# Attention results turned by VectorE in squares of 32 instead of by TensorE

## The chip, the cores and the metric

The kernel runs on one core of a Trainium2 chip. The time is that of one execution on the device in microseconds (us); it is given as the median of several runs. PE is TensorE (matmuls, and PEld its weight loads), DVE is VectorE, ACT is ScalarE, POOL is GpSimd, SP issues the DMAs.

## The reference

256 tokens of 2048 channels go through one block with pooling and gated linear attention and a feed-forward layer, and then through two layers of a second block. The change lies in these two layers. Each computes, in float32:

```
h = rmsnorm(x);  z = h @ w_in                   # latents, conv inputs, q_mem, gate
q = rope(rmsnorm(q_lat) @ w_uq)                 # 8 heads of 128 + 64
k, v = rmsnorm(kv_lat) @ w_ukv
a_out = softmax(q k^T * scale) @ v              # 8 heads, v of 128 channels
c_out = gated convolution over 3 tokens         # 512 channels
m_out = softmax(q_mem mk^T * scale) @ mv        # 4 heads against 256 memory tokens
y = concat(a_out, c_out, m_out) * silu(gate)
x = x + rmsnorm(y @ w_o)
```

## The kernel before

**The stream.** Every product with a weight matrix is a group of k tiles (128 rows of weights, up to 512 columns). A float32 product is made of three matmuls of reduced precision: weights and activations are split into a high part (`wh`, a copy by ACT) and a low part (`wl`, the rest, by DVE), and PE computes high x high, low x high, high x low (L997 to L999). One k tile is a step; a 512-wide step is 6 matmuls for the two halves of 128 tokens. Weights are loaded in slabs of two k tiles, and there are four buffers of split slabs, so ACT may split a slab when PE has done the slab four before it. The results of a group lie in one of two PSUM accumulators, `pm`; a group may start when the group two before it has been taken out of PSUM (by ACT or DVE, as the group says).

**The background.** Everything else, attention too, is written on each engine as a generator that yields the step at which its next piece is due. On PE a piece due at step d is issued before step d. On ACT and DVE pieces are put between the splits of slabs; since these run ahead of PE, a piece due at step d stands before the split of the slab that begins six steps after d (d rounded up to even). All engines run their instructions in order, so a piece that waits holds all that is behind it.

**Attention.** A layer has 12 heads: 4 against the memory and then 8 of the sequence, two at a time (lanes `ln` 0 and 1), in six rounds r. `ROUNDS[r]` gives the steps one, two, three, four of a round, counted from the layer's first step L:

```python
ROUNDS = ((56, 60, 63, 69), (70, 74, 77, 81), (96, 100, 103, 107), (118, 122, 125, 129), (140, 144, 147, 151),
          (158, 162, 165, 169))
```

- one: PE computes the scores of both lanes into banks `pb` 4 and 5; DVE takes the row maxima (L1737), ACT the exponentials into `P` (L1096), with the sums; DVE their reciprocals.
- two: PE turns `P` (4 transposes of 128x128 for a lane, L654) into banks 6 and 7; DVE copies them to `PT` (L1746).
- three: PE multiplies by v (L836); DVE multiplies the result by the reciprocal and the gate and writes it over the first 128 columns of each half of `P` (L1755, due at three + 2; semaphore `ys`).
- four: PE turns this result, tokens on partitions, to channels on partitions (2 transposes for a lane); ACT copies it as the high part `yTh` (L1104, due at four + 1), DVE subtracts to get the low part `yTl` (L1557, due at four + 1).

`yT` is the activation of the last groups of a layer, `o`, which begin at step L + 184. The round of the last two heads is r = 5.

**Around it.** The groups of a layer are ql 0 to 15, kv, qm, gt3 48 to 63, uq0 64 to 67, gt0 68 to 83, uq1 84 to 87, ukv0 88 and 89, gt1 90 to 105, uq2 106 to 109, ukv1 110 and 111, gt2 112 to 127, uq3 128 to 131, ukv2, gc 134 to 149, ukv3 150 and 151, xi 152 to 167, gb, o. ACT takes out the gates gt (with a table load for Silu), uq (`s`, L1072), gc, and of ukv the values `vt` (L1138) and the high part of the keys `kT` (L1140); DVE takes the low part of the keys (L1846). DVE's rope of uq0 (L1684 to L1691) is due at step 68. Round r + 2 scores need `kT` of ukv r, so round 5's need that of ukv3. The feed-forward layer already turns its activations with DVE, in 16 instructions of 32 partitions x 256 elements (L1529), a block row of 4 at a time.

Of the kernel before, what the change touches and what calls it, by code (L numbers as in the profile page):

```python
# [7 lines left out]
F32 = mybir.dt.float32  # L8
F32R = mybir.dt.float32r
I32 = mybir.dt.int32  # L10
ACT = mybir.ActivationFunctionType
# [3 lines left out]
T = 256  # L15
# [256 lines left out]
def buffers(nc, ctx):  # L272
# [3 lines left out]
    def at(name, shape, off, dt=F32):  # L276
        return nc.alloc_sbuf_tensor_at(name, shape, dt, offset=base + int(off * 1024))

    def halves(name, nk, off_h, off_l):
        return at(name + "h", [128, nk, T], off_h, F32R), at(name + "l", [128, nk, T], off_l, F32R)  # L280
# [82 lines left out]
    m.vt = at("vt", [128, 2, 8, 128], RC + 36)  # L363
    m.gates = [at(f"gt{i}", [128, 2, 512], RC + 44 + 4 * i) for i in range(4)]
    m.S2 = [at(f"s2{i}", [128, 2, 512], RC + 60 + 4 * i) for i in range(2)]
    m.P = [at("P0", [128, 2, T], 4.5), at("P1", [128, 2, T], 6.5)]
    m.PT = [at("PT0", [128, 2, T], 8.5), at("PT1", [128, 2, T], 216)]
    m.kpeT = halves("kpeT", 1, 10.5, 218)
    m.kpd = at("kpd", [128, 2, 128], 218)
    m.rope_o = at("rope_o", [128, 2, 128], 219)  # L370
# [72 lines left out]
def ready(p, act, k, layer):  # L443

    if act in ("hT", "x2T", "xT3"):
        n = {"hT": 0, "x2T": 0, "xT3": 16 * (layer + 1)}[act]
        return ("hT_l" if act == "hT" else "xt_l"), n + k + 1
    if act in ("paT", "oT"):
        return act + "_l", k + 1
    if act == "mixT":  # L450
        return "mix_l", k // 2 + 1
    if act in ("memT", "memA", "memB"):
        return "mem_l", k // 4 + 1 if act == "memT" else {"memA": 4, "memB": 20}[act] + k + 1
    if act in ("qlT", "kvT"):
        return act[:2] + "_l", (4 if act == "qlT" else 2) * layer + k + 1
    if k in (8, 9, 10, 11):
        return "c_l", 2 * layer + (k - 8) // 2 + 1
    r, ln = ((k - 12) // 2, k % 2) if k >= 12 else (2 + k // 2, k % 2)
    return "y_l", 12 * layer + 2 * r + ln + 1


def sync_program(nc, s, m, a, cst, cpool, gains, out, p):
# [23 lines left out]
    def memory_again(n):  # L486

        for c in range(4):
            yield p.first[MEM_FROM[n]] + MEM_LOADS[n][c]
            if n:  # L490
                w.wait_ge(s["mm"], p.end["mv1"])
                w.wait_ge(s["yt_t"], 12)
            if c >= 2:
                w.wait_ge(s["mem_l"], 16 * n + 4 + 4 * (c - 1))
            elif n == 0 and c == 1:
                w.wait_ge(s["f_l"], 22)
            e.dma_start(m.memS[n][c % 2][:, :, :], a["memT"][:, 4 * c:4 * c + 4, :]).then_inc(s[f"d_m{c}"], 16)
# [140 lines left out]
def tensor_program(nc, s, m, p):  # L638
# [148 lines left out]
    def attention(l, r, which):  # L787

        idx = 2 * (6 * l + r)
        if which == 0:  # L790
            j = r % 2
            for ln in range(2):
                free(4 + ln)
            if r < 2:
                w.wait_ge(s["qm_l"], 2 * l + r + 1)
                w.wait_ge(s["mk_l"], l + 1)
                w.wait_ge(s["ev_a"], p.evac[f"mv{l}"])
                for ln in range(2):
                    h = 2 * r + ln
                    for qh in range(2):  # L800
                        o, qs = pb[4 + ln][:, qh * T:qh * T + T], slice(qh * 128, qh * 128 + 128)
                        e.matmul(o, m.qmT[0][:, h, qs], m.mkS[0][:, h, :], start=True, stop=False)
                        e.matmul(o, m.qmT[0][:, h, qs], m.mkS[1][:, h, :], start=False, stop=False)
                        ins = e.matmul(o, m.qmT[1][:, h, qs], m.mkS[0][:, h, :], start=False, stop=True)
                    ins.then_inc(s["sc"], 1)
            else:
                w.wait_ge(s["uq_l"], 4 * l + r - 1)
                w.wait_ge(s["uqr_l"], 2 * (4 * l + r - 1))
                w.wait_ge(s["kp_l"], l + 1)
                w.wait_ge(s["ev_d"], p.evac[f"ukv{l}{r - 2}"])  # L810
                (qh_, ql_), (kh_, kl_) = m.qT[j], m.kT[j]
                for ln in range(2):
                    for qh in range(2):
                        o, qs = pb[4 + ln][:, qh * T:qh * T + T], slice(qh * 128, qh * 128 + 128)
                        e.matmul(o, qh_[:, ln, qs], kh_[:, ln, :], start=True, stop=False)
                        e.matmul(o, qh_[:, ln, qs], kl_[:, ln, :], start=False, stop=False)  # L816
                        e.matmul(o, ql_[:, ln, qs], kh_[:, ln, :], start=False, stop=False)  # L817
                        e.matmul(o, m.qTr[j][ln][:, 0, qs], m.kpeT[0][:, 0, :], start=False, stop=False)  # L818
                        ins = e.matmul(o, m.qTr[j][ln][:, 0, qs], m.kpeT[1][:, 0, :], start=False, stop=True)
                    ins.then_inc(s["sc"], 1)  # L820
        if which == 1:
            for ln in range(2):
                free(6 + ln)
                w.wait_ge(s["ex"], 2 * (idx + ln) + 2)
                for kk in range(2):
                    ins = turn(6 + ln, kk, [m.P[ln][:, qh, kk * 128:kk * 128 + 128] for qh in range(2)])
                ins.then_inc(s["pt_t"], 1)
                bank[6 + ln] = ("pt_c", idx + ln + 1)
        if which == 2:
            for ln in range(2):  # L830
                h = 2 * r + ln if r < 2 else 2 * (r - 2) + ln
                w.wait_ge(s["pt_c"], idx + ln + 1)
                for qh in range(2):
                    for kk in range(2):
                        v = m.mv[l][:, kk, h * 128:h * 128 + 128] if r < 2 else m.vt[:, kk, h, :]
                        ins = e.matmul(pb[4 + ln][:, qh * 128:qh * 128 + 128], m.PT[ln][:, kk, qh * 128:qh * 128 + 128], v,  # L836
                                       start=(kk == 0), stop=(kk == 1))
                ins.then_inc(s["pv"], 1)
                bank[4 + ln] = ("ys", 2 * (idx + ln) + 2)
        if which == 3:  # L840
            for ln in range(2):
                free(6 + ln)
                w.wait_ge(s["ys"], 2 * (idx + ln) + 2)
                turn(6 + ln, 0, [m.P[ln][:, qh, 0:128] for qh in range(2)]).then_inc(s["yt_t"], 1)
                bank[6 + ln] = ("y_l", idx + ln + 1)

    def uq_turn(l, j):
        S = m.S2[S2_OF[f"uq{j}"]]
# [169 lines left out]
def scalar_program(nc, s, m, xT, lead, p):  # L1018
# [20 lines left out]
    def view(b, n=2):  # L1039
        return m.pb[b][:, 0:n * T].rearrange("p (n t) -> p n t", t=T)  # L1040
# [45 lines left out]
    def attention(l, r, which):  # L1086
        idx = 2 * (6 * l + r)
        if which == 0:
            for ln in range(2):
                nb, ls = m.lane[ln][1], m.lane[ln][2]  # L1090
                scale = 128.0 ** -0.5 if r < 2 else 192.0 ** -0.5
                w.wait_ge(s["mx"], 2 * (idx + ln) + 2)
                if idx:
                    w.wait_ge(s["yt_t"], idx + ln - 1)
                for qh in range(2):
                    e.activation(m.P[ln][:, qh, :], m.pb[4 + ln][:, qh * T:qh * T + T], ACT.Exp, bias=nb[:, qh:qh + 1],  # L1096
                                 scale=scale, accum_out=ls[:, qh:qh + 1]).then_inc(s["ex"], 1)
        if which == 1:
            for ln in range(2):
                k = 12 + 2 * r + ln if r < 2 else 2 * (r - 2) + ln  # L1100
                if k in (6, 7):
                    w.wait_ge(s["mm"], p.end[f"ukv{l}3"])
                w.wait_ge(s["yt_t"], idx + ln + 1)
                e.activation(m.yT[0][:, k:k + 1, :], view(6 + ln, 1), ACT.Copy).then_inc(s["y_h"], 1)  # L1104

    def uq_taken(l, j):
        key = f"uq{j}"
# [65 lines left out]
    def layer(l):  # L1173
# [61 lines left out]
        gate_taken(l, 3)  # L1235
        yield p.end[f"uq{l}0"]
        uq_taken(l, 0)
        yield L + ROUNDS[0][3] + 1
        attention(l, 0, 1)
        yield L + ROUNDS[1][0] + 2  # L1240
        attention(l, 1, 0)
        uq_copy(l, 0)
        yield L + UQ_R[0] + 1
        uqr_copy(l, 0)
        yield L + ROUNDS[1][3] + 1
        attention(l, 1, 1)
        yield p.end[f"gt{l}0"]
        gate_taken(l, 0)
# [8 lines left out]
        for rr in range(2, 6):  # L1257
# [5 lines left out]
            if rr == 4:  # L1263
# [1 line left out]
                w.wait_ge(s["uq_t"], 4 * l + 4)  # L1265
                w.wait_ge(s["rp"], RP[f"uq{l}3"])
                taken(0, f"gc{l}", m.S2[0], scale=f"r{r}")
            yield L + ROUNDS[rr][3] + 1
            attention(l, rr, 1)
            if rr < 4:  # L1270
                yield p.end[f"uq{l}{rr}"]
# [238 lines left out]
def vector_program(nc, s, m, p):  # L1510
# [218 lines left out]
    def attention(l, r, which):  # L1729
        idx = 2 * (6 * l + r)  # L1730
        scale = 128.0 ** -0.5 if r < 2 else 192.0 ** -0.5
        for ln in range(2):
# [15 lines left out]
            if which == 3:  # L1748
# [5 lines left out]
                for qh in range(2):  # L1754
                    e.scalar_tensor_tensor(m.P[ln][:, qh, 0:128], m.pb[4 + ln][:, qh * 128:qh * 128 + 128], rl[:, qh:qh + 1],  # L1755
                                           m.gates[g][:, qh, (h % 4) * 128:(h % 4) * 128 + 128], ALU.mult, ALU.mult
                                           ).then_inc(s["ys"], 1)
            if which == 4:
                k = 12 + 2 * r + ln if r < 2 else 2 * (r - 2) + ln
                low(6 + ln, m.yT, k, 1, "y_h", n + 1, "y_l")  # L1760

    def uq_low(l, j):
        low(6, m.qT[j % 2], 0, 2, "uq_c", 4 * l + j + 1, "uq_l")
# [17 lines left out]
    def layer(l):  # L1781
# [26 lines left out]
        for r in range(6):  # L1808
# [9 lines left out]
            attention(l, r, 2)  # L1818
            yield three + 2
            attention(l, r, 3)  # L1820
            if r == 1:
                yield L + UQ_R[0] + 1
                uqr_low(l, 0)
# [3 lines left out]
            if r == 5:  # L1827
# [4 lines left out]
                for half in range(2):  # L1832
                    e.scalar_tensor_tensor(m.S2[0][:, half, :], acc[:, half, :], m.rs[f"r{l + 1}"][:, half:half + 1],
                                           m.S2[0][:, half, :], ALU.mult, ALU.mult).then_inc(s["ev_d"], 1)
            yield four + 1
            attention(l, r, 4)
            if 1 <= r <= 3:
                yield p.end[f"uq{l}{r}"]
# [428 lines left out]
```

## Time and profile before

| what | value |
|---|---|
| median of 3 runs | 2307.06 us (2307.02 to 2307.28) |
| the profiled execution's own time | 2307.33 us |
| its span, first to last instruction | 2305.5 us |
| PE, PEld busy | 2294.6 us (100%), 1925.8 us (84%) |
| DVE, ACT, POOL busy | 1463.2 us (63%), 1173.9 us (51%), 25.5 us (1%) |
| granted TensorE clock | 0.999 of full speed |
| HBM read | 434.99 MB, 190 GB/s over the span |
| layer 0, layer 1: first matmul | at 1540.95 us, 1930.99 us |

Busy time counts an instruction from its start to its end; matmuls overlap, so the distance between the starts of two of them, not their length, is what one costs on PE. The rows below come from queries of the same execution; their times are us from the span's start. In a row of a timeline, "x4" means that four instructions were merged, and brackets at the end give the idle time of the engine just before and what ended it.

### The profile page before, as it was taken

The page shows a single profiled execution, that of the slowest core. Times are in us where ns is not written, and L with a number is a line of the kernel's source. Part 1 is how long each engine was busy: PE and PEld are TensorE (multiplying, and loading weights), DVE is VectorE, ACT ScalarE, POOL GpSimd, SP SyncE. Part 2 cuts the span into 40 slices and gives each one's busy share as a digit, 9 for nine tenths or more (in the row PEclk, how much of TensorE's full clock was granted, in tenths as well). Part 3 has the DMA queues.
Part 4 walks back from the last instruction along what each step waited for, and adds up shares of the span by engine and source line. Part 5 has one row for each costly group of instructions (what it writes and reads, how often), then busy time and mean ns, then how long its engine had stood idle before and what let it go on. Part 6 is the DMA issues. An engine that isn't in the chain of part 4 may idle for free.

```text
span 2305.5 us, 27392 instructions
## 1 busy us (share of the span) xinstructions
PE 2294.6 (100%) x10829; PEld 1925.8 (84%) x10829; DVE 1463.2 (63%) x1969; ACT 1173.9 (51%) x1549; POOL 25.5 (1%) x35
## 2 busy tenths in 40 slices
PE   9999999999999999999999999999999999999998
PEld 7888888888888888888888888888888888888887
DVE  6677777756666666676467566675555755565565
ACT  6555655444445744444444444465655446565443
POOL 0000000000000000000000000000000000000000
PEclk9999999999999999999999999999999999999999
DMA  9666665766667566666666666756555665655564
GB/s 295 179 190 200 195 186 168 225 202 202 193 206 267 175 195 196 192 193 195 188 199 192 193 191 217 228 167 195 157 158 157 212 216 147 204 157 156 159 202 136
DMA packets 243983, 443.08 MB, mean 192 GB/s; under 512 B 18736, under 2 KB 48944, under 8 KB 243216
## 3 DMA queue, kind: packets, MB, share of 16 engines
q1 hardware_dynamic: 243424, 440.81, 63.2%
q8 instruction: 85, 1.39, 0.2%
q10 hardware_dynamic: 432, 0.53, 0.1%
q14 instruction: 42, 0.34, 0.1%
HBM read 434.99 MB, written 2.10 MB: 190 GB/s over the span
## 4 chain that ended last, share of the span: by engine, by line
PE 98%; DVE 1%; ACT 0%; DMA 0%; SPq 0%; issue 0%; DVEq 0%; ACTq 0%
PE pm L997 30%; PE pm L999 30%; PE pm L998 30%; PE pb L654 2%; PE pb L836 1%; PE pb L734 1%; PE pb L744 0%; DMA raw<-in_w_in 0%; DVE wl L2192 0%; PE pb L818 0%; PE pb L816 0%; PE pm L991 0%; PE pm L992 0%; PE pm L986 0%; PE pb L817 0%; PE pm L990 0%
## 5 line engine op out<-in xcount | busy, mean ns | idle before, releaser
L2192 DVE TENSOR_TENSOR wl<-raw,wh 128x1024 fp32r<-128x1024 f32 (+3 forms) x786 | 948.6, 1211 | 717.6 <-ACT wh L1501 714.6
L1501 ACT ACTIVATE wh<-raw 128x1024 fp32r<-128x1024 f32 (+3 forms) x786 | 819.8, 1046 | 909.0 <-PE pm L999 904.7
L997 PE MATMUL pm<-wh,hTh 128*128 128x512 f32 x702 | 275.5, 392 | 1.4 <-DVE wl L2192 1.3
L998 PE MATMUL pm<-wl,x2Th 128*128 128x512 f32 x704 | 274.2, 389 | 0.0
L999 PE MATMUL pm<-wh,x2Tl 128*128 128x512 f32 x704 | 274.2, 389 | 0.0
L997 PE MATMUL pm<-wh,x2Th 128*128 128x512 f32 x704 | 274.1, 389 | 0.0
L999 PE MATMUL pm<-wh,hTl 128*128 128x512 f32 x702 | 273.6, 390 | 0.0
L998 PE MATMUL pm<-wl,hTh 128*128 128x512 f32 x702 | 273.6, 390 | 0.0
L997 PE MATMUL pm<-wh,xT3h 128*128 128x512 f32 (+1 forms) x640 | 251.2, 392 | 0.0
L999 PE MATMUL pm<-wh,xT3l 128*128 128x512 f32 (+1 forms) x640 | 245.1, 383 | 0.0
L998 PE MATMUL pm<-wl,xT3h 128*128 128x512 f32 (+1 forms) x640 | 244.8, 382 | 0.0
L997 PEld LDWEIGHTS pm<-wh,hTh 128*128 128x128 f32 x702 | 131.9, 188 | 29.5 <-DVE wl L2192 3.2
L998 PEld LDWEIGHTS pm<-wl,x2Th 128*128 128x128 f32 x704 | 132.2, 188 | 27.4
L997 PEld LDWEIGHTS pm<-wh,x2Th 128*128 128x128 f32 x704 | 132.2, 188 | 27.4
L999 PEld LDWEIGHTS pm<-wh,x2Tl 128*128 128x128 f32 x704 | 132.2, 188 | 27.3
L999 PEld LDWEIGHTS pm<-wh,hTl 128*128 128x128 f32 x702 | 131.8, 188 | 27.6
L998 PEld LDWEIGHTS pm<-wl,hTh 128*128 128x128 f32 x702 | 131.9, 188 | 26.5
L999 PEld LDWEIGHTS pm<-wh,xT3l 128*128 128x128 f32 x640 | 120.2, 188 | 23.3
L998 PEld LDWEIGHTS pm<-wl,xT3h 128*128 128x128 f32 x640 | 120.6, 188 | 19.7
L997 PEld LDWEIGHTS pm<-wh,xT3h 128*128 128x128 f32 x640 | 120.5, 188 | 19.6
L997 PE MATMUL pm<-wh,yTh 128*128 128x512 f32 x240 | 93.8, 391 | 0.0
L999 PE MATMUL pm<-wh,yTl 128*128 128x512 f32 x240 | 93.5, 390 | 0.0
(423 smaller groups left out, 3205.6 us busy)
## 6 DMA issues: line engine op xcount, KB each, us to landing
raw<-in_w_in SPq DMA_DIRECT2D x286, 512.0 KB, 3.8
raw<-in_w_ffn_gate SPq DMA_DIRECT2D x88, 512.0 KB, 4.4
raw<-in_w_ffn_up SPq DMA_DIRECT2D x88, 512.0 KB, 4.4
raw<-in_w_ffn_down SPq DMA_DIRECT2D x88, 512.0 KB, 4.2
raw<-in_w_o SPq DMA_DIRECT2D x64, 512.0 KB, 4.3
raw<-in_w_in SPq DMA_DIRECT2D x68, 256.0 KB, 3.5
raw<-in_w_branch_b SPq DMA_DIRECT2D x32, 512.0 KB, 3.8
raw<-in_w_out SPq DMA_DIRECT2D x32, 512.0 KB, 4.6
```

Of the source, the lines that this page charges most:

```text
L654: ins = e.transpose(pb[b][:, o:o + 128], src[half], ident[:, :])
L734: ins = e.matmul(pb[4 + i][:, j * 128:j * 128 + 128], E[:, 4 * i + j, 0, ft, :], E[:, 4 * i + j, 1, ft, :], start=(ft == 0), stop=(ft == 1))
L836: ins = e.matmul(pb[4 + ln][:, qh * 128:qh * 128 + 128], m.PT[ln][:, kk, qh * 128:qh * 128 + 128], v, start=(kk == 0), stop=(kk == 1))
L997: e.matmul(o, ah[:, kk, t], h[:, c], start=first, stop=False)
L998: e.matmul(o, ah[:, kk, t], l[:, c], start=False, stop=False)
L999: ins = e.matmul(o, al[:, kk, t], h[:, c], start=False, stop=last)
L1501: e.activation(h[:, 0:n], r[:, 0:n], ACT.Copy).then_inc(s["hi"], 1)
L2192: e.tensor_tensor(l[:, 0:n], r[:, 0:n], h[:, 0:n].bitcast(F32), ALU.subtract).then_inc(s["lo"], 1)
```

## The change

In rounds 0 to 4 of each layer PE no longer turns the results. `P` of the two lanes becomes one buffer `PP`, and DVE turns both heads in 16 instructions, each of which takes a block row of 32 tokens and a block column of 32 channels, for both heads and both halves, and writes 32 partitions of the new buffer `yR` in SBUF. They are due at three + 2 to three + 5. ACT's copy (both heads at once, 128x512, from `yR`) becomes due at three + 7, DVE's subtraction (both heads at once) at three + 8. `yt_t` and `y_l` now count 7 a layer instead of 12. ACT's exponentials of a round wait for the transposes of the round before, as they read `P`. Round 5 is left on PE.

```diff
@@ buffers
-    m.P = [at("P0", [128, 2, T], 4.5), at("P1", [128, 2, T], 6.5)]
+    m.PP = at("PP", [128, 2, 2, T], 4.5)
+    m.P = [m.PP[:, ln, :, :] for ln in range(2)]
+    m.yR = at("yR", [128, 2, T], 2.5)
@@ tensor_program, attention
-        if which == 3:
+        if which == 3 and r == 5:
             for ln in range(2):
                 free(6 + ln)
                 w.wait_ge(s["ys"], 2 * (idx + ln) + 2)
                 turn(6 + ln, 0, [m.P[ln][:, qh, 0:128] for qh in range(2)]).then_inc(s["yt_t"], 1)
-                bank[6 + ln] = ("y_l", idx + ln + 1)
+                bank[6 + ln] = ("y_l", 7 * l + r + ln + 1)
@@ scalar_program, attention
                 if idx:
-                    w.wait_ge(s["yt_t"], idx + ln - 1)
+                    w.wait_ge(s["yt_t"], 7 * l + r if r else 7 * l - 1 + ln)
...
+        if which == 1 and r < 5:
+            k = 12 + 2 * r if r < 2 else 2 * (r - 2)
+            w.wait_ge(s["yt_t"], 7 * l + r + 1)
+            e.activation(m.yT[0][:, k:k + 2, :], m.yR[:, :, :], ACT.Copy).then_inc(s["y_h"], 1)
@@ scalar_program, layer (rounds 0, 1 and 2 to 5)
-        yield L + ROUNDS[0][3] + 1
+        yield L + ROUNDS[0][2] + 7
         attention(l, 0, 1)
...
-            yield L + ROUNDS[rr][3] + 1
+            yield L + ROUNDS[rr][2] + 7 if rr < 5 else L + ROUNDS[rr][3] + 1
@@ vector_program, attention
+        if which == 4 and r < 5:
+            k = 12 + 2 * r if r < 2 else 2 * (r - 2)
+            w.wait_ge(s["y_h"], 7 * l + r + 1)
+            e.tensor_tensor(m.yT[1][:, k:k + 2, :], m.yR[:, :, :], m.yT[0][:, k:k + 2, :].bitcast(F32), ALU.subtract
+                            ).then_inc(s["y_l"], 1)
+
+    def results_turned(l, r, at0):
+
+        yield at0
+        w.wait_ge(s["ys"], 2 * (2 * (6 * l + r) + 2))
+        for a in range(4):
+            yield at0 + a
+            for c in range(4):
+                ins = e.transpose(m.yR[32 * c:32 * c + 32, :, :].rearrange("p n (h a t) -> p n h a t", h=2, a=4)[:, :, :, a, :],
+                                  m.PP[32 * a:32 * a + 32, :, :, 32 * c:32 * c + 32])
+        ins.then_inc(s["yt_t"], 1)
@@ vector_program, layer
             yield three + 2
             attention(l, r, 3)
+            if r < 5:
+                yield from results_turned(l, r, three + 2)
...
-            yield four + 1
+            yield three + 8 if r < 5 else four + 1
             attention(l, r, 4)
```

## Rows read from the trace of the kernel before

**Rows 1.** The page: the chain that ended last, by engine.

```profile
PE 98%; DVE 1%; ACT 0%; DMA 0%; SPq 0%; issue 0%; DVEq 0%; ACTq 0%
```

**Rows 2.** Who waited for whom on PE, whole span (total us, times, longest us).

```profile
PE pm L997 <- DVE wl L2192: 1.3, 2, 1.0
```

**Rows 3.** Timeline of PE, layer 0, round 2's turn of results (start, length, engine, line).

```profile
1696.47 0.34 PE L999 MATMUL pm<-wh,qlTl 128*128 128x384 f32 x1
1696.65 0.60 PE L654 MATMUL pb<-ident,P 128*128 128x128 f32 x4
...
1697.26 0.34 PE L998 MATMUL pm<-wl,qlTh 128*128 128x384 f32 x1
```

**Rows 4.** Groups by line, DVE, each shape apart (busy us, mean ns, idle before).

```profile
L1529 DVE STREAM_TRANSPOSE turned<-fst 32x256 f32<-32x256 f32 x176 | 76.7, 436 | 2.8
...
L1534 DVE STREAM_TRANSPOSE sqq<-stg 128x1024 f32<-128x1024 f32 x4 | 5.0, 1239 | 0.0
```

**Rows 5.** Timeline of DVE, a turn of the feed-forward layer.

```profile
851.48 1.78 DVE L1529 STREAM_TRANSPOSE turned<-fst 32x256 f32<-32x256 f32 x4
853.28 1.23 DVE L2192 TENSOR_TENSOR wl<-raw,wh 128x1024 fp32r<-128x1024 f32 x1
854.54 1.80 DVE L1529 STREAM_TRANSPOSE turned<-fst 32x256 f32<-32x256 f32 x4
```

**Rows 6.** Timeline of DVE, layer 0, rounds 0 and 1; last row layer 1.

```profile
1631.48 1.23 DVE L2192 TENSOR_TENSOR wl<-raw,wh 128x1024 fp32r<-128x1024 f32 x1 [4.39 <-ACT wh L1501]
1632.62 1.12 DVE L1755 SCALAR_TENSOR_TENSOR P<-pb,st,gt 128x128 f32<-128x128 f32 x4
...
1634.79 0.29 DVE L1684 TENSOR_TENSOR rt<-s,cosT 128x128 f32<-128x128 f32 x1
...
1636.00 1.23 DVE L2192 TENSOR_TENSOR wl<-raw,wh 128x1024 fp32r<-128x1024 f32 x1
1637.14 0.76 DVE L1557 TENSOR_TENSOR yTl<-pb,yTh 128x256 fp32r<-128x256 f32 x2
...
1638.94 0.69 DVE L1737 TENSOR_REDUCE st<-pb 128x2 f32<-128x512 f32 x1
...
2029.90 0.69 DVE L1737 TENSOR_REDUCE st<-pb 128x2 f32<-128x512 f32 x1
```

**Rows 7.** Timeline of ACT, layer 0, exponentials of round 1, end of each lane.

```profile
1640.69 0.20 ACT L1096 ACTIVATION_READ_ACCUMULATOR P<-pb,st 128x1 f32 x1
...
1641.58 0.21 ACT L1096 ACTIVATION_READ_ACCUMULATOR P<-pb,st 128x1 f32 x1
```

**Rows 8.** Timeline of PE, layer 0: the four starts that wait for others.

```profile
1643.84 1.03 PE L654 MATMUL pb<-ident,P 128*128 128x128 f32 x8
...
1665.09 0.28 PE L984 MATMUL pm<-kvTh,wh 128*128 128x256 f32 x1
...
1703.10 0.40 PE L997 MATMUL pm<-wh,xT3h 128*128 128x512 f32 x1
...
1777.40 0.28 PE L815 MATMUL pb<-kT1h,qT1h 128*128 128x256 f32 x1
```

**Rows 9.** Timeline of DVE, layer 0: the multiplies of rounds 1, 2 and 4.

```profile
1654.01 1.12 DVE L1755 SCALAR_TENSOR_TENSOR P<-pb,st,gt 128x128 f32<-128x128 f32 x4
...
1695.36 1.12 DVE L1755 SCALAR_TENSOR_TENSOR P<-pb,st,gt 128x128 f32<-128x128 f32 x4
...
1765.68 1.12 DVE L1755 SCALAR_TENSOR_TENSOR P<-pb,st,gt 128x128 f32<-128x128 f32 x4
```

**Rows 10.** Timeline of ACT, layer 0: table load and gates, uq2, values of ukv3.

```profile
1659.50 1.28 ACT L1072 ACT_TABLE_LOAD   x1
...
1661.10 1.27 ACT L1072 ACTIVATE gt<-pm,st 128x512 f32<-128x512 f32 x2 [0.32 <-PE pm L999]
...
1700.50 1.05 ACT L1072 ACTIVATE s<-pm,st 128x384 f32<-128x384 f32 x2 [1.00 <-PE pm L999]
...
1769.41 0.60 ACT L1138 ACTIVATE vt<-pm 128x512 f32<-128x512 f32 x1 [0.49 <-PE pm L992]
```

More of the change, by code:

```diff
@@ L458, in ready @@
     r, ln = ((k - 12) // 2, k % 2) if k >= 12 else (2 + k // 2, k % 2)
-    return "y_l", 12 * layer + 2 * r + ln + 1
+    return "y_l", 7 * layer + r + 1 + (r == 5 and ln)
 def sync_program(nc, s, m, a, cst, cpool, gains, out, p):
@@ L491, in memory_again @@
                 w.wait_ge(s["mm"], p.end["mv1"])
-                w.wait_ge(s["yt_t"], 12)
+                w.wait_ge(s["yt_t"], 7)
             if c >= 2:
@@ L1097, in attention @@
                                  scale=scale, accum_out=ls[:, qh:qh + 1]).then_inc(s["ex"], 1)
-        if which == 1:
-            for ln in range(2):
[L1100 to L1104, printed above, removed]
+        if which == 1 and r < 5:
+            k = 12 + 2 * r if r < 2 else 2 * (r - 2)
+            w.wait_ge(s["yt_t"], 7 * l + r + 1)
+            e.activation(m.yT[0][:, k:k + 2, :], m.yR[:, :, :], ACT.Copy).then_inc(s["y_h"], 1)
+        elif which == 1:
+            for ln in range(2):
+                w.wait_ge(s["mm"], p.end[f"ukv{l}3"])
+                w.wait_ge(s["yt_t"], 7 * l + r + ln + 1)
+                e.activation(m.yT[0][:, 6 + ln:7 + ln, :], view(6 + ln, 1), ACT.Copy).then_inc(s["y_h"], 1)
     def uq_taken(l, j):
@@ L1244, in layer @@
         uqr_copy(l, 0)
-        yield L + ROUNDS[1][3] + 1
+        yield L + ROUNDS[1][2] + 7
         attention(l, 1, 1)
@@ L1757, in attention @@
                                            ).then_inc(s["ys"], 1)
-            if which == 4:
-                k = 12 + 2 * r + ln if r < 2 else 2 * (r - 2) + ln
-                low(6 + ln, m.yT, k, 1, "y_h", n + 1, "y_l")
+            if which == 4 and r == 5:
+                low(6 + ln, m.yT, 6 + ln, 1, "y_h", 7 * l + r + ln + 1, "y_l")
+        if which == 4 and r < 5:
[12 more added lines that the diff above has]
+        ins.then_inc(s["yt_t"], 1)
     def uq_low(l, j):
```

## The prediction

> **What bounds the kernel now.** I read the page first. The chain that ended last is PE for 98% of the span [rows 1]: what PE does not do is gained at once, and what PE has to wait for is lost at once. Next the view of who waits: after start-up PE's matmuls of the weight stream waited 1.3 us in all, twice [rows 2]. So there is no idle time on PE to recover; the change can only take PE work away, or put waits in. 0.2% of 2307 us, 4.6 us, is about what a measurement of this kernel can tell from no change.
>
> Then the timelines around the change. In each attention round DVE and ACT have their own work between weight splits, and PE meets the results at fixed steps. What decides is by how much each result is early today: for each round I put the last DVE or ACT instruction that PE waits for beside PE's start. The second layer is the first one again, 390.96 us later (its maximum starts 2029.90, the first layer's 1638.94 [rows 6]), so I work out the first and double it.
>
> **What is removed.** Rounds 0 to 4 of two layers lose four PE transposes each, 40 in all. Around such a group [rows 3] two matmul starts that would be 0.18 us apart each stand from 1696.47 to 1697.26: 0.79 - 0.36 = 0.43 us. The group costs 0.11 us a transpose, not the 0.60 us that its row seems busy, because the records overlap. In a stretch of 512-wide matmuls the next gaps are also some ns wider; that bounds a group by 0.49. I take 0.45, so 10 x 0.45 = **4.5 us off PE** (bounds 4.3 and 4.9). If everything else were hidden this alone is the result, 0.19%.
>
> **What is added on DVE.** 16 transposes of 32 partitions x 128 elements a round. The trace has this operation at 256 and at 1024 elements, 436 and 1239 ns [rows 4]. A straight line through them has (1239 - 436)/768 = 1.05 ns an element and 168 ns fixed, so 128 elements take 302 to 304 ns. Their starts are 1.80/4 = 0.45 us apart, 0.014 more than one is busy [rows 5], where the six small rope instructions of 0.29 us between 1634.79 and 1636.00 start 1.21/6 = 0.20 us apart [rows 6]. So transposes do not overlap: a pace of 0.304 + 0.014, taken as 0.319 us. Lower bound: half of the 256-element pace, 0.22 (the fixed part gone, or overlap after all). Upper bound: 0.45 (no gain from the smaller size). It is nearest to the line, since both rows are the same operation. 16 x 0.319 = **5.1 us a round**. A split is followed by the next ordinary instruction after 1.14 us [rows 6], 0.09 before its own end, but by a transpose after 1.26 [rows 5]. Two subtractions from PSUM (0.76 us) become one of 512 elements (0.69, as the maximum of that size, and 0.60 to the next start) [rows 6]. ACT's two copies of a round become one; I leave it at the same length.
>
> The Trainium skill, "VectorE: DVE Perf Modes", section on the TRN2 errata, speaks against this change: an SBUF-source instruction of this engine has a fixed cost whatever its length, which it measures at about 150 cycles, so many small tiles pay it many times. Its figure would make 290 ns of a 128-element instruction; the sum would be 2318 instead of 2320. The same page, section on two Vector instructions with no wait between them, says that an instruction whose output starts in another group of 32 partitions than the one before is held until all earlier ones have finished. The 0.45 us pace agrees; without that rule the sum would be that of the short transposes below.
>
> **Where it lies in the queues.** In DVE's program an item due at step d stands ahead of the split of the slab that begins six steps after d (d rounded up to even). The results' multiply (due at three + 2) and 8 transposes thus come before one split and 8 before the next, without a gap in DVE's work. ACT's copy waits for the last of them, and ACT's next evacuations and splits are queued behind it. DVE catches up before every next round; before round 0's multiply its split had waited 4.39 us for ACT [rows 6]. So each round is a case of its own. A resumed PE starts some 0.13 us after its releaser ends, my allowance (bounds 0 and 0.25, one matmul's pace).
>
> *Round 0.* DVE has no gap from the multiply at 1632.62 to round 1's maximum at 1638.94 [rows 6]. New order and starts: multiply 1632.62 (1.12, and 0.04 until its own result can be read), transposes 1633.78, split 1636.33, transposes 1637.59, rope 1640.14, split 1641.35, split 1642.49, subtraction 1643.63, maximum 1644.23. (ACT's copy starts at 1640.2 and its next split is done by 1641.8, so it holds nobody.) The maximum is 5.29 late. ACT's exponentials follow it: lane 0 done 1640.89, lane 1 1641.79 today [rows 7], then 1646.18 and 1647.08. PE wants lane 0 at 1643.84 [rows 8] less 0.45, 1643.39. It starts at 1646.31, does 4 transposes (0.44), waits for lane 1 until 1647.21 and ends at 1647.65, not 1644.27: 3.38 us. The chain behind (copy of q, two splits, reciprocals, DVE's copy of PT) then just misses the next product by 0.1. **3.5 us.**
>
> *Round 1.* Multiply 1654.01 [rows 9], transposes from 1655.17, a split of 768 elements (1.0), the last transpose ends 1661.26. ACT's copy (0.52), a table load (1.3) and the gates (1.27) follow, which are done 1664.38 instead of 1662.37 [rows 10]. PE's group ukv0 needs them at 1665.09 - 0.45 = 1664.64 [rows 8], less 0.13 of resumption: 0.13 us to spare. **0.**
>
> *Rounds 2 and 3.* Multiply 1695.36 [rows 9], transposes from 1696.52, split at 1699.07, transposes 1700.33 to 1702.88. Behind them on ACT stand the copy (0.52 to the next start) and the evacuation of uq, which so moves from 1700.50 [rows 10] to 1703.43 and ends 1.05 later, 1704.48. PE's group gt2 may not start before that (every group waits for the evacuation of the one two before it), and wants to at 1703.10 - 0.45 = 1702.65 [rows 8]. 1704.61 - 1702.65 = **1.96 us**, and the same in round 3, whose rows stand 35.16 later: 3.9 together.
>
> *Round 4.* Multiply 1765.68 [rows 9], last transpose ends 1773.20. ACT's vt copy moves from 1769.41 [rows 10] to 1773.75 and the split behind it ends 1775.8; on DVE split, subtraction and then the low part of kT, done 1778.24. PE's scores of round 5 want it at 1777.40 - 0.45 = 1776.95 [rows 8]: 1778.37 - 1776.95 = **1.42 us**. Round 5 is as before.
>
> **The sum.** A layer: 3.5 + 0 + 3.9 + 1.4 = 8.8; two: 17.7. Less 4.5: **+13.2 us**. The profiled execution took 2307.33, so 2320.5; the median of the runs is 0.27 lower, so **2320.3**. Every 0.01 us of a transpose's pace moves each of four rounds by 0.16 and the total by 1.3 us. The terms move together: at 0.22 the rounds cost 1.9, 0, 0.4, 0.4 and 0, and the total is +0.9 (2308); at 0.45 (round 1 then counts 2.0) +34 (2341). An error of 0.3 us in the margins of four rounds twice is 2.4 us.
>
> **The rivals.**
> (a) *All hidden, faster.* DVE is busy 63% of the span and its splits are made slabs ahead of PE, so the transposes fit on average. That holds if the 16 transposes delay DVE little enough. From the sum: PE breaks even when the delay shrinks by 1.72 us, at 3.4 us for 16, 0.21 us each; below about 1.6 us for 16 nothing waits. At that end 2302.6. Against it: no transpose in the trace is near this, and DVE's work in round 0 has no gap.
> (b) *Short transposes.* Overlap, or little fixed cost: pace 0.22 to 0.27, time 2307 to 2314. For it: rope's small instructions do overlap. Against it: the transposes of the trace that don't [rows 5].
> (c) *The clock falls.* The longest wait of PE becomes 2.9 us with another shortly behind it; after start-up none is over 1.0 us today [rows 2], at a granted clock of 1.00 (2.4 GHz). If it fell to 1.2 GHz behind both, a step of 1.36 us would take at most twice as long; three steps in each layer are 8 us, 2328. The Trainium skill, "TensorE: Matmul & The Clock Gate", rules for kernel authors, warns of long idle gaps of PE between bursts of matmuls; no row here shows one.
> (d) *Size does not matter to a transpose.* 0.45 each, 2341. That 1024 elements take 2.8 times as long as 256 [rows 4] speaks against it.
>
> **How the numbers follow.** The sum as it stands, 2314 to 2327: 0.66. (b) in its part below 2314: 0.13. (a): 0.08. (c): 0.08. (d): 0.05. The likeliest case has 2320.3, own range 2314 to 2327. The range for 8 in 10 has to take in most of (b), whose bound is 2308, and some of (c): 2308 to 2328. Faster by over 0.2% (below 2302.4) needs (a) with 4.7 us or more off PE; I give faster 0.06, most of (a), since the hidden case lies on the line. Same, 2302.4 to 2311.7: the rest of (a) and most of (b), 0.13. Slower: 0.81.
>
> **What would show it.** DVE transposes of about 304 ns, 0.32 apart, 160 of them; PE with 40 fewer transposes and four waits a layer: before the turns of P in round 1 (on ACT's P), before gt2 and gc (on ACT's s), before the scores of round 5 (on DVE's kT low part); none in round 1 at the gates. Wrong if the transposes are shorter than 0.27, if DVE's order around step 65 to 71 is not the one above, or if PE's waits name anything else.

## The result

| kernel | median | all its runs |
|---|---|---|
| before | 2307.11 us | 2307.02 to 2307.28, 4 runs |
| after | 2328.18 us | 2327.66 to 2328.62, 4 runs |

After is slower by a factor of 1.0091 (95% interval 1.0074 to 1.0109), 21.1 us. The direction was as predicted, and so was the mechanism in rounds 1 to 4. The size was not: 13.2 us were worked out, and 2328.2 lies just above the range of 2308 to 2328. In round 0 PE waited for another instruction than the forecast had.

The page of after, busy time of each engine, and the chain that ended last:

```profile
PE 2296.6 (99%) x10789; PEld 1925.7 (83%) x10789; DVE 1510.6 (65%) x2119; ACT 1172.8 (50%) x1539; POOL 25.5 (1%) x35
...
PE 93%; DVE 4%; ACT 1%; issue 1%; DMA 0%; SPq 0%; DVEq 0%; ACTq 0%
```

DVE has only 47 us more to do, in a span with some 840 us in which it is idle, and yet it now has 4% of a chain in which it had 1% [rows 1]. That share is no price, for PE's new waits for DVE are 12.0 us in all; the waits and the experiments below tell what was lost. Who waits for whom on PE, in after (total us, times, longest us):

```profile
PE pb L657 <- DVE qT0l L1562: 9.6, 2, 4.8
PE pm L1000 <- ACT s L1075: 6.7, 4, 1.7
PE pb L818 <- DVE kT1l L1868: 2.4, 2, 1.2
PE pm L1000 <- DVE wl L2214: 1.5, 3, 0.6
```

The first three of these lines are new against [rows 2]. The second and the third are the waits forecast for rounds 2, 3 and 4. The first stands where the forecast had a wait for ACT's exponentials, but it names another releaser: DVE's `qT0l`, the low part of the queries uq0. It is twice 4.8 us, not twice 2.9.

**The size of a transpose.** After's DVE group and its timeline in round 0, which answers to [rows 4] and [rows 6]:

```profile
L1778 DVE STREAM_TRANSPOSE yR<-PP 32x128 f32<-32x128 f32 x160 | 48.5, 303 | 2.6
```

```profile
1632.63 1.12 DVE L1760 SCALAR_TENSOR_TENSOR PP<-pb,st,gt 128x128 f32<-128x128 f32 x4
1633.78 2.51 DVE L1778 STREAM_TRANSPOSE yR<-PP 32x128 f32<-32x128 f32 x8
1636.31 1.22 DVE L2214 TENSOR_TENSOR wl<-raw,wh 128x1024 fp32r<-128x1024 f32 x1
1637.57 2.53 DVE L1778 STREAM_TRANSPOSE yR<-PP 32x128 f32<-32x128 f32 x8
...
1641.34 2.35 DVE L2214 TENSOR_TENSOR wl<-raw,wh 128x1024 fp32r<-128x1024 f32 x2
1643.61 0.68 DVE L1768 TENSOR_TENSOR yTl<-yR,yTh 128x512 fp32r<-128x512 f32 x1
1644.21 0.69 DVE L1742 TENSOR_REDUCE st<-pb 128x2 f32<-128x512 f32 x1
...
1647.59 0.69 DVE L1562 TENSOR_TENSOR qT0l<-pb,qT0h 128x512 fp32r<-128x512 f32 x1 [1.69 <-ACT qT0h L1125]
```

Eight transposes take 2.53 us, 0.316 each; 0.319 was taken. Each start down to the maximum at 1644.21 lies within 0.02 us of the one worked out (1644.23). The last row is the instruction that was missed.

**Where PE stopped, and what came behind.** Timeline of PE in after, same place; the row at 1648.34 answers to the first of [rows 8]:

```profile
1643.14 0.39 PE L1002 MATMUL pm<-wh,xT3l 128*128 128x512 f32 x1
1648.34 1.97 PE L657 MATMUL pb<-ident,PP 128*128 128x128 f32 x8 [4.81 <-DVE qT0l L1562]
1649.96 0.78 PE L1000 MATMUL pm<-wh,xT3h 128*128 128x512 f32 x1
1650.53 0.63 PE L1001 MATMUL pm<-wl,xT3h 128*128 128x512 f32 x1
1650.96 0.63 PE L1002 MATMUL pm<-wh,xT3l 128*128 128x512 f32 x1
...
1652.66 0.49 PE L1000 MATMUL pm<-wh,xT3h 128*128 128x512 f32 x1
1652.99 0.40 PE L1001 MATMUL pm<-wl,xT3h 128*128 128x512 f32 x1
1653.23 0.39 PE L1002 MATMUL pm<-wh,xT3l 128*128 128x512 f32 x1
...
1654.14 0.39 PE L1000 MATMUL pm<-wh,xT3h 128*128 128x512 f32 x1
```

In a full stream the next matmul starts 0.23 us behind the one before. Here, behind the idle stretch, they stand 0.43 apart (1650.53, 1650.96), and only from 1652.99 on again 0.24. The windows of after show the same by the clock (us of the window, busy us and instructions of PE, PEld, DVE, ACT and POOL, granted clock, DMA share, GB/s):

```profile
1640.00:1644.00 4.00, 3.52 (x16) 2.58 (x14) 3.97 (x10) 2.87 (x3) 0.00 (x0) 1.00 0.13 31
1644.00:1648.00 4.00, 0.00 (x0) 0.00 (x0) 2.24 (x6) 2.86 (x10) 0.00 (x0) 0.76 0.63 221
1648.00:1652.00 4.00, 3.67 (x13) 3.28 (x14) 3.75 (x7) 1.45 (x2) 0.00 (x0) 0.50 0.24 46
1652.00:1656.00 4.00, 4.00 (x20) 3.33 (x19) 0.73 (x2) 1.06 (x1) 0.00 (x0) 0.89 0.63 217
```

A clock of 0.50 is the lower level, 1.2 GHz instead of 2.4; 0.76 and 0.89 are windows with a change of level in them, the first of them all idle on PE. So round 0 costs more than its wait. Step 76 of the layer starts with the matmul at 1654.14. In the kernel before it started at 1647.48:

```profile
1647.48 0.39 PE L997 MATMUL pm<-wh,xT3h 128*128 128x512 f32 x1
```

That is 6.7 us later, although the turn of round 0's results is gone from PE. The last matmul before the wait, at 1643.14, would have had its successor at 1643.37, so the wait took 4.97 us. The turn's eight transposes hold the stream for 1.62 us (1648.34 to 1649.96) instead of 0.79 (1643.84 to 1644.63), 0.8 us, and the stretched gaps up to 1652.99 add 1.3: 2.2 us by the clock. In the second layer the wait is the same and eleven gaps are stretched instead of seven: 3.0 us. The lower level itself stands for the same 6.8 us in both layers. In the second it sets in nearer to the start of the turn (1648.34 in the first layer, 2049.55 in the second), so that more of it falls on work:

```profile
1646.10:1652.80 6.70, 4.46 (x15) 3.89 (x16) 4.38 (x7) 3.35 (x8) 0.00 (x0) 0.50 0.41 129
...
2048.90:2055.60 6.70, 6.05 (x19) 5.09 (x20) 4.28 (x7) 1.76 (x2) 0.00 (x0) 0.50 0.48 133
```

**Rounds 2 and 4.** Timelines of after: ACT's copy and the evacuation of uq2 behind it (third of [rows 10]), and the two PE starts that answer to the last two of [rows 8]:

```profile
1709.04 0.63 ACT L1104 ACTIVATE yTh<-yR 128x512 fp32r<-128x512 f32 x1 [3.84 <-DVE yR L1778]
1709.58 1.03 ACT L1075 ACTIVATE s<-pm,st 128x384 f32<-128x384 f32 x2
```

```profile
1710.66 0.50 PE L1000 MATMUL pm<-wh,xT3h 128*128 128x512 f32 x1 [1.68 <-ACT s L1075]
...
1787.47 0.36 PE L818 MATMUL pb<-kT1h,qT1h 128*128 128x256 f32 x1 [1.22 <-DVE kT1l L1868]
```

ACT stands 3.84 us for the transposes with the evacuation queued behind it, and PE stands for the evacuation: the chain as forecast. Beside the same matmuls of the kernel before, PE's start slips by 1.84 us in rounds 2 and 3 and by 1.38 in round 4, and some matmuls later the stream has fallen back by 1.95 and 1.45 (forecast 1.96 and 1.42). Each of these waits left the clock at 1.00, as the windows around two of them show:

```profile
1708.00:1714.00 6.00, 4.32 (x26) 3.56 (x25) 4.60 (x11) 4.92 (x8) 0.00 (x0) 1.00 0.57 169
...
1784.00:1794.00 10.00, 8.79 (x48) 7.40 (x48) 6.23 (x9) 5.85 (x12) 0.00 (x0) 1.00 0.70 211
```

### The profile page after: what moved, and what is told of

It is laid out like the page before. It is cut to its first block, busy times and chain, and to the rows that moved or that the text cites. A ratio compares the mean times of both kernels' runs of the same rounds, so it can differ in the third digit from the quotient of the medians.

```text
span 2326.8 us, 27450 instructions
## 1 busy us (share of the span) xinstructions
PE 2296.6 (99%) x10789; PEld 1925.7 (83%) x10789; DVE 1510.6 (65%) x2119; ACT 1172.8 (50%) x1539; POOL 25.5 (1%) x35
## 4 chain that ended last, share of the span: by engine, by line
PE 93%; DVE 4%; ACT 1%; issue 1%; DMA 0%; SPq 0%; DVEq 0%; ACTq 0%
PE pm L1000 29%; PE pm L1002 29%; PE pm L1001 29%; PE pb L657 2%; DVE yR L1778 2%; DVE wl L2214 1%; PE pb L839 1%; PE pb L737 1%; ACT wh L1506 1%; DVE PP L1760 0%; PE pb L747 0%; DMA raw<-in_w_in 0%; PE pb L818 0%; ACT s L1075 0%; PE pb L821 0%
```

## The experiments

Two theories stood after the result. *By parts*: round 0 costs 7.5 us a layer (7.1 and 7.9), made of a wait of 5 for PSUM bank 6, into which PE turns `P`, and a fall of the clock, and rounds 2 to 4 cost what was predicted. *By the clock alone* (the rival of the prediction): the wait is the one predicted and the fall of the clock makes all the rest.

| kernel | what is different from after | median us | ratio to before (95%) |
|---|---|---|---|
| r0_on_pe | round 0 left on PE | 2314.23 | 1.0031 (1.0019 to 1.0043) |
| filled | the idle stretch ahead of round 1's turn of `P` filled with matmuls | 2323.39 | 1.0071 (1.0056 to 1.0086) |
| uq_turn_later | bank 6 taken by uq0 only behind the turn of `P` | 2324.41 | 1.0076 (1.0061 to 1.0091) |
| act_order | rounds 2 to 4: evacuations ahead of the copy | 2316.64 | 1.0041 (1.0027 to 1.0055) |
| r0_pe_order | r0_on_pe and act_order together | 2303.72 | 0.9985 (0.9976 to 0.9994) |
| best | all five rounds on DVE, reordered | 2303.04 | 0.9982 (0.9973 to 0.9991) |
| only_r1 | round 1 alone on DVE | 2306.53 | 0.9997 (0.9988 to 1.0006) |
| r1_24 | 24 transposes instead of 16 in round 1 | 2332.02 | 1.0108 (1.0094 to 1.0121) |

Before had 2307.16 us beside the first four and 2307.22 beside the last four.

**r0_on_pe: what round 0 costs in all.** Rounds 1 to 4 stay on DVE; rounds 0 and 5 are turned by PE as in the kernel before.

```diff
+DV = (1, 2, 3, 4)
...
-        if which == 3 and r == 5:
+        if which == 3 and r not in DV:
...
-        yield L + ROUNDS[0][2] + 7
+        yield L + ROUNDS[0][2] + 7 if 0 in DV else L + ROUNDS[0][3] + 1
```

> Round 0 of each layer goes back to PE, rounds 1 to 4 stay on DVE. The traces of before and after, laid over each other step by step, put 7.1 us (layer 0) and 7.9 us (layer 1) of lost time between steps 70 and 76, less the 0.5 us that round 0's own group gave. If each round is a case of its own (theory), 14 us come back: 2314.1 us, with a granted clock of 1.00 throughout and the four waits on ACT's s and DVE's kT as they are. Rival: the loss is one of DVE's total load, so a fifth of it comes back: about 2324.

2314.23 us: 13.95 less than after. So round 0 costs 7.0 us a layer net, where 3.5 less 0.45 were predicted, and the other rounds together come out as predicted: 2 x 5.3 of waits less 8 x 0.45 is +7.1, and 7.07 were measured. PE's waits of this kernel lack the first line and keep the two others:

```profile
PE pm L1008 <- ACT s L1083: 6.7, 4, 1.7
PE pb L826 <- DVE kT1l L1879: 2.4, 2, 1.2
```

**filled: what the clock costs.** While it would stand idle, PE multiplies parts of the memory's keys, which lie in SBUF, into bank 7. Nobody reads the product.

```diff
+        if which == 1 and r == 1:
+            free(7)
+            for _ in range(20):
+                e.matmul(pb[7][:, :], m.mkS[0][:, 0, 0:128], m.mkS[0][:, 0:2, :], start=True, stop=True)
```

> The changed kernel with 20 matmuls of 128x512 without use (into bank 7, which is then written by the turn of lane 1) put on PE ahead of round 1's turn of P, where PE otherwise stands idle for 5.0 us. They take 20 x 0.227 = 4.5 us, so they end before the turn may start. Theory: the 1.2 GHz stretches behind the two waits (7 and 11 matmul gaps of 0.427 us and the turns at half speed, 2.2 and 3.0 us) come from that idle time; the clock stays at 1.00 and the time falls by 5.2 us to 2323.0. Rival: the low clock has another cause (the turns themselves, or what follows), then the time stays at 2328 or grows.

2323.39 us, 4.8 less than after, with work added. Timeline and windows of PE in this kernel:

```profile
1642.94 4.70 PE L827 MATMUL pb<-mkSh 128*128 128x512 f32 x20
1647.92 1.09 PE L657 MATMUL pb<-ident,PP 128*128 128x128 f32 x8 [0.29 <-DVE qT0l L1566]
1648.77 0.48 PE L1004 MATMUL pm<-wh,xT3h 128*128 128x512 f32 x1
1649.09 0.40 PE L1005 MATMUL pm<-wl,xT3h 128*128 128x512 f32 x1
```

```profile
1648.00:1652.00 4.00, 4.00 (x22) 3.44 (x23) 3.68 (x6) 1.15 (x3) 0.00 (x0) 1.00 0.38 104
```

The turn still waits for the same subtraction and starts 4.98 us after its turn came (1642.94), but the clock is 1.00 behind it and the stream goes on at once. The fall of the clock is thus some 4.8 us of the total (5.2 by the rows of after), and the wait of 5 us is there without it: the clock does not explain everything.

**uq_turn_later: is it the bank?** PE's turn of uq0, the user of bank 6 before the turn of `P`, is put behind that turn (step 78 instead of 71), and so are its copy and its subtraction.

```diff
@@ tensor_program, round 1
-                if r == 1 and which == 0:
-                    yield L + UQ_N[0]
-                    uq_turn(l, 0)
                 if r == 1 and which == 2:
+                    yield L + 78
+                    uq_turn(l, 0)
```

> The changed kernel with the turn of uq0 on PE moved from step 71 to step 78, behind round 1's turn of P and product, and its copy by ACT and subtraction by DVE with it. Theory: round 1's turn of P waits today for bank 6, which is free only when DVE has subtracted uq0's low part (ends 1648.28), not for the exponentials of lane 0 (end 1646.16). Then PE starts it about 1646.3, 2 us earlier, lane 1 follows the exponentials at 1647.1, and the net gain is about 1.5 us a layer. If the shorter idle time also spares the clock, 2328.2 - 3.1 - 5.2 = 2319.9; if the clock falls all the same, 2325. Rival: the exponentials alone hold PE: no change, 2328.

2324.41 us, 3.8 less than after. PE's timeline in this kernel:

```profile
1642.53 0.39 PE L1001 MATMUL pm<-wh,xT3l 128*128 128x512 f32 x1
1646.09 2.03 PE L657 MATMUL pb<-ident,PP 128*128 128x128 f32 x8 [3.17 <-ACT PP L1098]
1647.77 0.78 PE L999 MATMUL pm<-wh,xT3h 128*128 128x512 f32 x1
1648.34 0.63 PE L1000 MATMUL pm<-wl,xT3h 128*128 128x512 f32 x1
```

Now the releaser is ACT's `PP`, the exponentials, at 1646.09, where the prediction had put PE's start at 1646.31. So the chain of the prediction is there; it was only not the last to arrive. Without the bank's wait the idle stretch is 3.3 us (1642.53 + 0.23 to 1646.09), 1.6 less in each layer, which is 3.3 of the 3.8 us; and the clock still falls to 1.2 GHz behind it (the first matmul holds the stream for 0.57 us instead of 0.31, and the next takes 0.63 instead of 0.39).

**act_order: the chain of rounds 2 to 4.** ACT's copy moves behind the evacuation of uq in rounds 2 and 3 and behind that of ukv3 in round 4; DVE's low part of the keys goes ahead of the results' in round 4.

```diff
@@ scalar_program, rounds 2 to 5
-            yield L + ROUNDS[rr][2] + 7 if rr < 5 else L + ROUNDS[rr][3] + 1
-            attention(l, rr, 1)
             if rr < 4:
                 yield p.end[f"uq{l}{rr}"]
                 uq_taken(l, rr)
+            if rr == 4:
+                yield p.end[f"ukv{l}{rr - 1}"]
+                ukv_taken(l, rr - 1)
+            yield L + ROUNDS[rr][2] + 7 if rr < 5 else L + ROUNDS[rr][3] + 1
+            attention(l, rr, 1)
-            if rr < 5:
+            if rr < 4:
                 yield p.end[f"ukv{l}{rr - 1}"]
                 ukv_taken(l, rr - 1)
...
```

> The changed kernel with ACT's copy of the turned results put behind the evacuation of uq (rounds 2 and 3) or of ukv3 (round 4), and in round 4 DVE's low part of kT put ahead of the low part of yT. Nothing is taken away. Theory: the waits before gt2 and gc (1.84 us each, twice) and before round 5's scores (1.38, twice) are ACT's and DVE's in-order queues, held by the copy that waits for the transposes; they vanish: 2328.2 - 10.1 = 2318.1. Rival: ACT and DVE are late there because DVE's splits are late: then PE waits for wl instead and less than half comes back, 2324 or more.

2316.64 us. The waits for `s` and `kT1l` are gone; of the change's waits this one is left:

```profile
PE pb L657 <- DVE qT0l L1565: 9.6, 2, 4.8
```

By the starts of the same matmuls in both traces the three rounds give back 1.95, 1.95 and 1.45 us a layer, 10.7 in all, and the two profiled executions differ by 10.6. The medians differ by 11.5. The executions of this kernel lie 2.5 us apart (2315.56 to 2318.05, the profiled one the slowest), so that a median of five can be off by such a difference; why they lie so far apart was not shown.

**r0_pe_order: both cures at once.** It tells whether the two parts add.

> Round 0 on PE and, for rounds 2 to 4, the orders of act_order: both repairs together, rounds 1 to 4 turned by DVE. Theory: the losses are separate and all accounted for, so 2314.2 - 10.1 = 2304.1 us, with no wait on PE in the two layers: 8 groups of four PE transposes less, at 0.38 to 0.5 us each, is 3.5 us below the kernel before. Rival: DVE's 28 extra busy us a kernel cost something even without a visible wait: 2306 or more.

2303.72 us, 3.5 less than before, with none of the change's waits left on PE. For rounds 1 to 4 the order alone makes the difference: the buffers are those of after. Eight groups off PE at 0.45 are 3.6.

**best: all five rounds, without a wait.** DVE writes the results to a buffer of their own, so that the exponentials need not wait for the transposes. Round 0's transposes stand behind round 1's copy of `PT`, the others four to eight between two splits, and copy and subtraction come late, behind the evacuations.

```diff
+    m.yP = [at(f"yP{l}", [128, 2, 2, 2, 128], 200 + 8 * l) for l in range(2)]
...
+            if r == 1:
+                yield from results_turned(l, 0, L + 76, (0, 1))
+                yield from results_turned(l, 0, L + 78, (2, 3))
...
+                yield from results_turned(l, 1, L + 84, (0, 1))
+                yield from results_turned(l, 1, L + 86, (2,))
+                yield from results_turned(l, 1, L + 88, (3,))
...
+            if r in (2, 3):
+                for a in range(3):
+                    yield from results_turned(l, r, three + 3 + 2 * a, (a,))
+                yield p.end[f"uq{l}{r}"]
+                uq_rope(l, r)
+                yield from results_turned(l, r, three + 9, (3,))
```

> All five rounds on DVE, but with the results written to a buffer of their own (so the exponentials need not wait for the transposes), round 0's transposes behind round 1's copy of PT, at most 4 or 8 in front of one split, ACT's copy and DVE's subtraction behind everything that PE waits for. Theory: the loss was only the place in the queues; nothing waits and 10 groups of PE transposes are saved: 2307.1 - 4.6 = 2302.5 us, clock 1.00. Rival: 5.2 us of DVE time a round do not fit beside splits and attention, and PE waits for wl, PT or the low part of kT somewhere: 2305 or more.

2303.04 us, 4.2 less than before and 25.1 less than after, with the same 160 transposes. Its group of transposes, and DVE's timeline in the same stretch as above:

```profile
L1783 DVE STREAM_TRANSPOSE yR<-yP 32x128 f32<-32x128 f32 x160 | 48.4, 303 | 2.7
```

```profile
1638.18 0.68 DVE L1747 TENSOR_REDUCE st<-pb 128x2 f32<-128x512 f32 x1
...
1641.56 0.69 DVE L1567 TENSOR_TENSOR qT0l<-pb,qT0h 128x512 fp32r<-128x512 f32 x1 [1.70 <-ACT qT0h L1126]
...
1645.57 1.28 DVE L1756 COPY PT<-pb 128x512 f32<-128x512 f32 x2
1646.76 2.50 DVE L1783 STREAM_TRANSPOSE yR<-yP 32x128 f32<-32x128 f32 x8
```

The transposes cost DVE the same 0.3 us each. The maximum and the subtraction are in time, since the transposes come only where nothing behind them is late for PE. In round 0 order and the buffer of its own were changed together; what the order alone would give there was not run.

**only_r1: the free round alone.** Rounds 0, 2, 3 and 4 are back on PE.

> Only round 1 is turned by DVE. By the rows of before it has 0.13 us to spare at the gates of ukv0, so PE does not wait and two groups of PE transposes are saved: 2307.1 - 1.0 = 2306.1 us. Rival: the margin is used up, then PE waits up to some tenths before ukv0 and the time is that of before or 2307.5.

2306.53 us: 0.7 less than before, no new wait on PE, as forecast for this round. By its interval this is no difference that can be told from none.

**r1_24: how far round 1's margin reaches.** After with eight transposes more in round 1, of the same size, into a buffer that nobody reads.

```diff
+            if r == 1 and a in (1, 2):
+                for c in range(4):
+                    e.transpose(
+                        m.spare[l][32 * c:32 * c + 32, :, :].rearrange("p n (h a t) -> p n h a t", h=2, a=4)[:, :, :, a, :],
+                        m.PP[32 * a:32 * a + 32, :, :, 32 * c:32 * c + 32])
```

> The changed kernel with 8 transposes of the same size and without use added to round 1's 16, ahead of the last eight. They cost 8 x 0.317 = 2.5 us of DVE. Theory: round 1 has some 0.13 us to spare and no more, since ACT's copy, table load and gates stand behind the last transpose; PE waits 2.4 us before ukv0 in both layers: 2328.2 + 4.8 = 2333.0. Rival: DVE stands idle over 3 us before round 1's multiply and 2 us before ukv0's neighbours, so the extra work is absorbed: 2328.

2332.02 us, 3.8 more than after, with a fourth wait, which names ACT's gates as the prediction's calculation of round 1 does:

```profile
PE pm L988 <- ACT gt L1076: 4.5, 2, 2.3
```

Eight times 0.316 is 2.5 us, and PE falls back by 2.4 in each layer: round 1 had all but no margin (0.1 us; 0.13 was worked out). That the total grew by 3.8 and not 4.8 goes with a shorter stretch at the lower clock: in this profile, 2.9 us above after's, round 0 costs 0.5 us less than in after in the first layer and 1.5 less in the second.

## Why the prediction was right and where it failed

| term | predicted | measured |
|---|---|---|
| PE's turns taken away, each | 0.45 us | 0.43 to 0.50, 2.3 a layer |
| pace of a DVE transpose | 0.319 us | 0.316 us |
| round 0, a layer | 3.5 us | 7.1 and 7.9 us |
| round 1, a layer | 0 | 0 |
| rounds 2 and 3, each | 1.96 us | 1.84 us at PE's start, 1.95 behind it |
| round 4 | 1.42 us | 1.38 us at PE's start, 1.45 behind it |

- *PE off, the transposes, DVE's order, rounds 1 to 4*: right, each from its own rows, and r0_on_pe shows their sum to 0.1 us. act_order shows the queues behind the waits of rounds 2 to 4.
- *Round 0, first failure*. "PE wants lane 0 at 1643.84 less 0.45 ... It starts at 1646.31": this took the data, `P`, for all that the turn waits for. The turn also needs a place to write. Bank 6 was last written by PE's turn of uq0 three steps before, and is free only when DVE's subtraction `qT0l` has read it; that stands behind ACT's copy `qT0h`, which stands behind both exponentials. In the kernel before the subtraction is done 0.83 us ahead of PE's start:

```profile
1642.32 0.69 DVE L1557 TENSOR_TENSOR qT0l<-pb,qT0h 128x512 fp32r<-128x512 f32 x1 [1.69 <-ACT qT0h L1120]
```

It moved with the maximum, by 5.27 us, and ends at 1648.28; PE starts at 1648.34. With PE 0.45 us earlier, round 0 had a margin of 0.4 us and not the 2.5 from 1640.89 to 1643.39. That costs 1.5 us a layer above the forecast, 3.0 in all, and uq_turn_later shows the releaser change, and the idle stretch shrink by 1.6 us, when this wait is taken away.

- *Round 0, second failure*: the sum has no term for the clock. The rival of the falling clock (0.08) was no alternative to the sum but came on top of it. It costs 2.2 and 3.0 us by the rows, 5.2 together, and 4.8 by filled. It needs one wait and not the two of the rival. The rival's 8 us for it and its 2328 us meet the measured time only because the bank's 3 us, which it did not have, stand in for what it had too much.
- *The sum*: 13.2 + 3.0 + 5.2 = 21.4 us, 21.1 measured.
- *All hidden* did not happen in after and is true of another order: best reaches 2303.04 with the transposes at their full price. The rival's 2302.6 was the right size for "no wait", but its condition, a delay below some 1.6 us for the 16, was too narrow. *Short transposes* and *size does not matter* fall with 0.303 us.

## What to carry to other kernels

When work is put into an in-order queue, list for each later instruction of the saturated engine all its conditions, the buffer or bank that it writes too, and write down each one's margin; the data's wait can be 2 us earlier than the bank's. Work for an engine that is idle a third of the time can still cost more than it saves: the same 160 instructions cost 21 us in one order and, in another and with a buffer of their own, gave 4. A forecast stall of several us on TensorE should carry a term for the clock behind it, as part of the main case and not as a rival.

## What the runs showed of the hardware

**One wait is enough for the clock, and what it costs varies.** A single idle stretch of 5.0 us (after) and one of 3.3 us (uq_turn_later) were each followed by 1.2 GHz; the six waits of up to 1.7 us in rounds 2 to 4 by none. In after, seven matmul gaps were stretched in the first layer and eleven in the second, behind waits of the same length and with the lower level standing for the same 6.8 us; in r1_24 it stood for 3.4 us in each layer. It need not set in while PE is idle: in the second layer of uq_turn_later PE starts again at 2046.38, and its windows are

```profile
2046.40:2048.10 1.70, 1.44 (x10) 1.16 (x11) 0.00 (x0) 1.70 (x6) 0.00 (x0) 1.00 0.47 178
2048.20:2051.50 3.30, 3.30 (x9) 2.53 (x9) 3.28 (x6) 0.94 (x1) 0.00 (x0) 0.50 0.26 55
```

The Trainium skill, "TensorE: Matmul & The Clock Gate", section "Why this matters for your kernels", warns of idle gaps of PE between bursts of matmuls. The traces here agree, and the same stretch filled with matmuls of no use kept the clock at 1.00 and the time 4.8 us lower.

**DVE transposes stand behind each other in full.** Eight of 303 ns take 2.51 to 2.53 us. The straight line through 256 and 1024 elements [rows 4] gave 302 to 304 ns for 128, though its two rows are of 32 and of 128 partitions. By that line 168 ns of each are fixed: an instruction of half the elements costs 303 ns and not half of 436.
